# A weight ring whose low halves are written over the raw values, with four slots for high halves

## The reference

```python
h = x + hybrid_mixer(rmsnorm(x), ...)      # u = n @ w_in, three mixers, each with a gate
h = h + peer_ffn(rmsnorm(h), ...)          # product-key retrieval of experts
out = rmsnorm(h)
# hybrid_mixer:
u_a, u_b, u_c, u_g = split(n @ w_in)       # n is 256 x 2048; w_in 2048 x 28,736
y_a = short_conv_mixer(u_a) @ w_branch_a
y_b = stick_breaking_attention(u_b) @ w_branch_b
y_c = mamba2_ssd(u_c, ...) @ w_branch_c    # SSD_WIDTH 4096
return (sigmoid(g_a) * y_a + sigmoid(g_b) * y_b + sigmoid(g_c) * y_c) @ w_out
```

## Time and profile before

| | |
|---|---|
| runs, median (lowest to highest) | 3657.72 us (3655.78 to 3658.47) |
| span of the profiled execution | 3653.4 us |
| TensorE busy | 3493.2 us (96%) |
| VectorE busy | 2281.0 us (62%) |
| ScalarE busy | 1774.5 us (49%) |
| share of the 16 DMA engines, main queue | 62.9% |
| TensorE idle before a matmul that waited for the ring's low half | 91.1 us, 49 times |

### The profile page before, as it was taken

The page is one execution under the profiler, slowest core; times in us unless marked ns, Lnnn a source line. Parts: engine busy times, 40 slices in busy tenths (PEclk is TensorE's granted clock), DMA queues, the critical chain, the costliest instruction groups (busy, mean ns, idle before and its releaser), DMA issues.

```text
span 3653.4 us, 70562 instructions
## 1 busy us (share of the span) xinstructions
PE 3493.2 (96%) x23289; PEld 3188.1 (87%) x23289; DVE 2281.0 (62%) x2906; ACT 1774.5 (49%) x2537; POOL 27.5 (1%) x32
## 2 busy tenths in 40 slices
PE   4999999999999999999999989999999999999998
PEld 4999788888789999987778989999999988888887
DVE  2555444444446777776455699988889955554555
ACT  3444434444434554555444533446777744444444
POOL 0000000000000000000000000000000000000000
PEclk8999999999999999999999999999999999999999
DMA  4666665555665455445667667676666677667765
GB/s 108 175 176 182 171 182 155 142 144 152 183 192 165 145 154 150 146 135 164 186 190 208 182 151 165 165 175 166 161 159 159 158 192 193 194 192 214 201 193 167
DMA packets 486714, 620.19 MB, mean 170 GB/s; under 512 B 80576, under 2 KB 345120, under 8 KB 485408
## 3 DMA queue, kind: packets, MB, share of 16 engines
q1 hardware_dynamic: 486560, 618.12, 62.9%
HBM read 613.62 MB, written 4.19 MB: 169 GB/s over the span
## 4 chain that ended last, share of the span: by engine, by line
PE 82%; DVE 7%; ACT 4%; issue 2%; DMA 2%; SPq 1%; DVEq 0%; ACTq 0%
PE bank L78 26%; PE bank L80 25%; PE bank L79 25%; PE bank L1673 3%; ACT f_hi L122 2%; DVE w_lo L1519 2%; DVE f_lo L127 2%; PE bank L2094 2%; DMA w_raw<-in_peer_down 1%; DVE w_raw L1512 1%; SPq L449 1%; DMA f_raw<-in_w_in 0%; SPq L524 0%; ACT L684 0%; DMA w_raw<-in_peer_up 0%
## 5 line engine op out<-in xcount | busy, mean ns | idle before, releaser
L127 DVE TENSOR_TENSOR f_lo<-f_raw,f_hi 128x768 fp32r<-128x768 f32 (+2 forms) x640 | 748.8, 1171 | 865.7 <-ACT f_hi L122 865.1
L122 ACT ACTIVATE f_hi<-f_raw 128x768 fp32r<-128x768 f32 (+2 forms) x640 | 648.4, 1015 | 934.8 <-PE bank L80 889.0
L78 PE MATMUL bank<-xT_hi,f_hi 128*128 128x256 f32 x2560 | 745.9, 291 | 92.3 <-DVE f_lo L127 75.2
L79 PE MATMUL bank<-xT_lo,f_hi 128*128 128x256 f32 x2560 | 724.9, 283 | 0.0
L80 PE MATMUL bank<-xT_hi,f_lo 128*128 128x256 f32 x2560 | 724.7, 283 | 0.0
L78 PE MATMUL bank<-xT_hi,w_hi 128*128 128x256 f32 x2048 | 591.2, 289 | 21.3 <-DVE w_lo L1519 21.3
L78 PEld LDWEIGHTS bank<-xT_hi,f_hi 128*128 128x128 f32 x2560 | 490.4, 192 | 110.0 <-DVE f_lo L127 44.3
L79 PE MATMUL bank<-xT_lo,w_hi 128*128 128x256 f32 x2048 | 578.9, 283 | 0.0
L80 PE MATMUL bank<-xT_hi,w_lo 128*128 128x256 f32 x2048 | 578.8, 283 | 0.0
L1611 DVE TENSOR_TENSOR w_lo<-w_raw,w_hi 128x1024 fp32r<-128x1024 f32 x256 | 313.6, 1225 | 340.5 <-PE bank L80 333.3
L79 PEld LDWEIGHTS bank<-xT_lo,f_hi 128*128 128x128 f32 x2560 | 491.3, 192 | 1.9 <-issue 1.7
(11 more groups left out here) (268 smaller groups left out, 4970.6 us busy)
## 6 DMA issues: line engine op xcount, KB each, us to landing
w_raw<-in_peer_down SPq DMA_DIRECT2D x1024, 128.0 KB, 3.6
w_raw<-in_peer_up SPq DMA_DIRECT2D x1024, 128.0 KB, 2.7
f_raw<-in_w_in SPq DMA_DIRECT2D x1024, 96.0 KB, 2.3
f_raw<-in_w_in SPq DMA_DIRECT2D x256, 256.0 KB, 2.9
f_raw<-in_w_in SPq DMA_DIRECT2D x384, 128.0 KB, 2.8
f_raw<-in_w_branch_c SPq DMA_DIRECT2D x256, 128.0 KB, 2.7
f_raw<-in_w_branch_a SPq DMA_DIRECT2D x128, 128.0 KB, 2.7
f_raw<-in_w_branch_b SPq DMA_DIRECT2D x128, 128.0 KB, 2.7
```

The lines of the kernel that those rows point to most:

```text
L78: nc.tensor.matmul(out, lhs[0], rhs[0], start=start, stop=False, skip_group_check=True)
L79: nc.tensor.matmul(out, lhs[0], rhs[1], start=False, stop=False, skip_group_check=True)
L122: nc.scalar.activation(self.hi[u % 2][:, 0:cols], self.raw[u % 4][:, 0:cols], ACT.Copy).then_inc(self.hi_done, 1)
L127: nc.vector.tensor_tensor(self.lo[u % 2][:, 0:cols], self.raw[u % 4][:, 0:cols], self.hi[u % 2][:, 0:cols].bitcast(F32), ALU.subtract).the ...
```

## The change

The low half of a unit is written over the raw values in the same slot, so four slots serve for raw and low together; the four slots that were two high and two low become four high ones. SP loads unit n when TensorE has used unit n-4 (it was: when the low half of n-4 was made), and ACT waits only for the raw values. The other edits replace the slot numbers.

```diff
             def __init__(self):
                 self.raw = [place(f"f_raw{i}", [P, SLOT // 4], at_ring + i * SLOT) for i in range(4)]
-                self.hi = [place(f"f_hi{i}", [P, SLOT // 4], at_ring + (4 + i) * SLOT, F32R) for i in range(2)]
-                self.lo = [place(f"f_lo{i}", [P, SLOT // 4], at_ring + (6 + i) * SLOT, F32R) for i in range(2)]
+                self.lo = [place(f"f_lo{i}", [P, SLOT // 4], at_ring + i * SLOT, F32R) for i in range(4)]
+                self.hi = [place(f"f_hi{i}", [P, SLOT // 4], at_ring + (4 + i) * SLOT, F32R) for i in range(4)]
...
             def room(self, sp, n):
                 if not (isinstance(n, int) and n < 4):
-                    sp.wait_ge(self.lo_done, n - 3)
+                    sp.wait_ge(self.used, n - 3)
 
             def split_hi(self, act, n, quads, u, cols):
 
                 act.wait_ge(self.raw_full[u % 4], (quads + u // 4 + 1) * 64)
-                if not (isinstance(n, int) and n < 2):
-                    act.wait_ge(self.used, n - 1)
-                nc.scalar.activation(self.hi[u % 2][:, 0:cols], self.raw[u % 4][:, 0:cols],
+                nc.scalar.activation(self.hi[u % 4][:, 0:cols], self.raw[u % 4][:, 0:cols],
                                      ACT.Copy).then_inc(self.hi_done, 1)
 
             def split_lo(self, dve, n, u, cols):
                 dve.wait_ge(self.hi_done, n + 1)
-                nc.vector.tensor_tensor(self.lo[u % 2][:, 0:cols], self.raw[u % 4][:, 0:cols],
-                                        self.hi[u % 2][:, 0:cols].bitcast(F32),
+                nc.vector.tensor_tensor(self.lo[u % 4][:, 0:cols], self.raw[u % 4][:, 0:cols],
+                                        self.hi[u % 4][:, 0:cols].bitcast(F32),
                                         ALU.subtract).then_inc(self.lo_done, 1)
...
-                                          (fl.hi[u % 2][:, at], fl.lo[u % 2][:, at]), (xT_hi[:, u, :], xT_lo[:, u, :]),
+                                          (fl.hi[u % 4][:, at], fl.lo[u % 4][:, at]), (xT_hi[:, u, :], xT_lo[:, u, :]),
```

More of the change, by code:

```diff
@@ L1732, in b_unit @@
                         tri_matmul(bank[m // 2][:, (m % 2) * T:(m % 2 + 1) * T],
-                                   (fl.hi[u % 2][:, at], fl.lo[u % 2][:, at]), xs,
+                                   (fl.hi[u % 4][:, at], fl.lo[u % 4][:, at]), xs,
                                    start=u == 0 and m % 2 == 0, stop=u == KD - 1)
@@ L1740, in b_unit @@
                         last = tri_matmul(V[:, tb * T:(tb + 1) * T], (xT_hi[:, u, t], xT_lo[:, u, t]),
-                                          (fl.hi[u % 2][:, at], fl.lo[u % 2][:, at]),
+                                          (fl.hi[u % 4][:, at], fl.lo[u % 4][:, at]),
                                           start=u == 0 and tb == 0, stop=u == KD - 1)
@@ L1892, in branch_unit @@
                                    (yT_hi[:, y0 + k, t], yT_lo[:, y0 + k, t]))
-                            last = tri_matmul(bank[pair[tb]][:, :], lhs, (fl.hi[m % 2][:, at], fl.lo[m % 2][:, at]),
+                            last = tri_matmul(bank[pair[tb]][:, :], lhs, (fl.hi[m % 4][:, at], fl.lo[m % 4][:, at]),
                                               start=k == 0, stop=k == (KD if kind == "g" else kb) - 1)
```

## The result

The changed kernel takes 3624.34 us (median of four executions) against 3657.34 us for the kernel before in the same measurement (3655.78 to 3658.47), 33 us less. One of the four ran at a mean granted clock of 0.791 in place of 0.991 and took 4094.48 us; it is left out of the ratio of 0.9905 (95% interval 0.9891 to 0.9919), and the other three took 3617.73, 3623.95 and 3624.72. 3633.5 was forecast, with a range of 3619 to 3652.

The account below looks back on a forecast made before the run. TensorE, busy 96% of the span, bounds the kernel, so only its waits can be won; +2.4 + 0.5 - 17.8 - 13.0 - 1.0 + 4.7 = -24.2 us takes the span to 3629.2, with 4.3 added 3633.5 us, range 3619 to 3652.

Parts of the forecast that it names:

- Loop in A: A: the way from a slot's use through refill and splits to the next first matmul, 8.51 us against four units' 8.64.
- A's term (+0.5): A: late landings cost an estimated 0.005 us per unit, 0.5 us in all; bounds -2 and +10.
- The rival of the refill: Whole kernel: refill sets the pace, so the change is slower, +15 us, 3673 us; chance 0.07.
- B, -17.8: B: seven iterations win 1.4 at unit 7 and 1.28 at unit 13, less 1 us for late loads; bounds 0 and -28.6.
- The rival in which the bursts do not move: B: bursts hang on TensorE's own matmuls, so B wins nothing; -6.4 us in all, 3651 us; chance 0.10.
- the one in which they are hidden whole: B and branch stages: a lead of two units throughout hides the bursts, -37.4 us in all, 3620 us; chance 0.10.
- Branch stages, -13.0: GA, GB, GC: high halves come about 1.0 us earlier; 16.6 won less 3.7 that stays; bounds 4 and 17.
- C, -1.0: C: loads cost nothing, unit 1's wait behind evacuate stays; 11.5 of 12.5 us stays, 1.0 won.
- Start, +2.4: Start: SP reaches d_col's loads later, so unit 16 starts 2.4 us later; bounds 0 and +3.
- O, +4.7: O: unit 10 starts 3.1 us later behind two 1 MB loads (+3.2), unit 3 adds +1.5; bounds 1 and 8.
- the +1.5 for unit 3: O: unit 3's load, behind f_keys, comes 3.1 us later, and half of that is lost, +1.5 us.
- Behind O, 0: Behind O: the PEER ring's first loads start 3 us later, covered by 4 us of unit work, so no loss.

Follow-up runs that it names:

- late_refill: Changed kernel, but SP refills a slot one unit later (unit n's load waits for the use of n-3, not n-4): 3891.12 us, ratio 1.0647.
- softplus_split: Changed kernel, but in B ACT's softplus is in two parts, behind the high halves of units 6 and 7, VectorE's part one unit later: 3617.43 us.
- two_ahead: Changed kernel with ACT's wait for TensorE's use of unit n-2 put back, slots and later refill kept: 3673.83 us, ratio 1.0044.
- three_ahead: Changed kernel, but ACT makes unit n's high half only after TensorE has used unit n-3: 3626.69 us, ratio 0.9913.
- evac_later: Changed kernel, but in C ACT does evacuate behind the high half of unit 1 of an iteration, not unit 0: 3608.14 us, ratio 0.9867.
- pool_small: Changed kernel, but GpSimd, not SP, issues the four small loads (dt_bias, dt_a_log, two of d_col) at the start: 3619.33 us, ratio 0.9892.
- row_d: Changed kernel, but d_col's values load as one contiguous row to every partition and VectorE spreads them with two copies in GA: 3589.10 us.
- acc_pieces: Changed kernel, but O's two 1 MB loads of acc become eight of 256 KB, spread from unit 5 to unit 29: 3614.24 us, ratio 0.9882.
- best: Changed kernel with d_col as a row, acc in eight pieces, evacuate behind unit 1 and softplus in two parts: 3555.54 us, ratio 0.9718.
- old_evac: Kernel before (two high slots), with only evacuate moved behind the high half of unit 1 in C: 3657.13 us, ratio 0.9995.

## Why the prediction was right, and where its terms were off

The mechanism and the sign are as forecast: a lead for ACT that hides part of each burst, paid for by a later refill. The forecast of -24.2 was 7 us short of -31.2.

- **Loop in A, 8.51 against 8.64 us.** Right: late_refill's 2.82 us per unit gives 3 x 2.82 = 8.46. A's term (+0.5) was -0.7 in sum, inside its bounds: the median step between units was 2.19 us before and is 2.16 now, so the old chain of splits cost a little that the forecast took for nothing. The rival of the refill is out: the median landing stayed at 2.4 us. The 2 us of HBM access at high load, which the prediction set beside it (the Trainium skill, DMA: Bandwidth & Descriptors, section "🔬 Latency and other measured facts") and by which it estimated 38 us lost in A, did not show as a longer landing here.
- **B, -17.8.** Measured -19.1. Unit 7 keeps a part, unit 8 all of its 0.32, unit 13 nothing; 16 waits where 14 were forecast, the two others, of 0.91 and 0.29 us, once each. The rival in which the bursts do not move is out, and so is the one in which they are hidden whole: a high half cannot be made before its slot is refilled, and only softplus_split, a change of order, got most of the rest.
- **Branch stages, -13.0.** Measured -22.1, the largest miss. The term that was mis-sized is what does not appear as a wait: the forecast put it at 1.2 us of short waits and took "which makes a unit of 12 about 2.76 us long" for TensorE's own pace. It was the pace under the old ring, read less than 2 us behind a wait. First matmuls of three units in a row in GB (338 to 340), in the kernel before:

```profile
939.76 0.43 PE L78 MATMUL bank<-f_hi,yT_hi 128*128 128x512 f32 x1
...
942.56 0.39 PE L78 MATMUL bank<-f_hi,yT_hi 128*128 128x512 f32 x1
...
945.33 0.43 PE L78 MATMUL bank<-f_hi,yT_hi 128*128 128x512 f32 x1
```

and the same units after:

```profile
913.99 0.39 PE L78 MATMUL bank<-f_hi,yT_hi 128*128 128x512 f32 x1
...
916.71 0.39 PE L78 MATMUL bank<-f_hi,yT_hi 128*128 128x512 f32 x1
...
919.42 0.39 PE L78 MATMUL bank<-f_hi,yT_hi 128*128 128x512 f32 x1
```

  2.80 and 2.77 us became 2.72 and 2.71; the median over GB's units fell from 2.77 to 2.72. The loss was too short to appear as idle time, since a matmul is drawn 0.39 long and follows in 0.23: it hid in the busy time, which in the three stages together fell by 11 of the 14 us. Take GB's steps between two of the ring's matmuls that show no idle time (some 760): in sum they exceed 0.2267 us each by 3.7 us in the kernel before, by 3.6 in two_ahead, by 0.7 in three_ahead and by 0.6 in the changed kernel. So the wait for unit n-2 makes it. GA's excess fell from 2.8 to 1.1 and GC's from 7.8 to 4.0, so 8.6 us of the 22 come from here; most of the rest, 11.5, is the waits that are drawn, with their 0.16 each. Why the steps inside a unit were longer too stays open.
- **C, -1.0.** Measured -1.7. Unit 1's wait hangs on ACT's order, shown by evac_later.
- **Start, +2.4.** Measured +2.0. A change of the issuer does not free unit 16 (pool_small), a contiguous row does (row_d).
- **O, +4.7.** Measured +6.9. The step "unit 10 starts 3.1 later" was too small: its wait was 1.0 us, was forecast at about 4 and is 5.7, and the sum left out that TensorE's clock falls in it, about 2 us more. Against that, the +1.5 for unit 3 was too much: it waits 0.52 us (0.68 lost).
- **Behind O, 0.** Measured +3.3. One wait of the PEER ring grew from 2.6 to 4.8 us, and again the clock is at its lower level for 6.8 us, from 2.5 us into the wait:

```profile
PE bank L78 <- DVE w_lo L1609: 4.8, 1, 4.8
...
3344.50:3351.40 6.90, 4.54 (x11) 3.58 (x12) 2.79 (x3) 3.47 (x4) 0.00 (x0) 0.51 0.88 225
```

  What made that wait longer, in a stage whose code is unchanged, was not tested. It differs from run to run: 2.5 us in acc_pieces and best, 3.0 to 3.3 in two_ahead, late_refill, row_d, evac_later and old_evac, 4.1 to 5.0 in three_ahead, softplus_split and pool_small.

## What to carry to other kernels

A ring is two numbers: how far its producers may run ahead, and how long the way is from "used" back to "ready" against slots times unit; work out the second before giving a slot to the first, and try it by taking one slot from the loop. Small losses can hide in the busy time, here 8.6 us in the branch stages, so take TensorE's own step from a stretch where nothing feeds it late. A longer ring does not move work that hangs in an engine's list behind something else; it makes a new order of that list pay (16 us). With the short ring the same order took 4.4 us of waits away and won no time, since the clock fell behind the waits that it made longer.

## What the runs showed of the hardware

- Two loads of 8 KB each whose elements of 4 bytes lie apart take some 32 us from issue to landing, whether SP or GpSimd issues them, and other loads all but stop meanwhile. Issued by GpSimd they go with a share of the DMA engines of 0.89 at 11 GB/s (20 to 40 us in pool_small), issued by SP with 0.05 at 0 GB/s (60 to 80 us in the changed kernel). A contiguous 32 KB load in their place lands in 4.3 us.
- In waits of 5.7 and 4.8 us the granted clock of TensorE fell to its lower level for 6.8 us, of which 4.5 lay behind the wait, and about 2.1 us were lost there each time. In evac_later and softplus_split unit 10's waits of 5.0 and 5.2 us had only 3.4 us of it. Waits of 1.8 to 2.1 us came with 3.4 us of it at some places and with none at others: the 2.11 us before unit 7 of B, three times of seven in old_evac and never in the kernel before. Between the wait for unit 16 and its end the kernel before has a single such stretch, 3.4 us behind a wait of 2.07 us. So an idle time on TensorE of some 5 us costs some 1.5 to 2.5 us more than itself.
- The median landing of a load did not change (2.4 us in A) when SP issued the loads later.
